# Expert gates: one-hots interleaved by two tokens, sixteen tokens an instruction, and gates stored token-innermost in chunks of 32

## What is computed

```python
idx = top-16 of (s_i + s_j) per head              # idx = i*128 + j, [t, 128 choices]
g   = softmax(best)                               # [t, 128]
a   = gelu(einsum('td,ted->te', xb, peer_u[idx]))
out = einsum('te,ted->td', (g * a), peer_v[idx])
```

## Time and profile before

| | |
|---|---|
| time, median of 3 runs | 4610.86 us (4606.46 to 4625.53) |
| profiled execution, its span | 4614.7 us |
| median against that span | 3.8 us below it |
| PE, DVE, ACT, POOL busy in the span | 3770.5, 3353.4, 1271.7, 989.7 us |
| up to `dense_gates` | 0 to 1976 us |
| `dense_gates` | 1976 to 2349 us, 373 us |
| `experts` | 2349 to 4562 us, 2213 us |
| `final_norm` | 4562 to 4614.7 us |

### The profile page before, as it was taken

One profiled execution on the slowest core, in us unless ns is written; L12 is line 12 of the kernel. 1 busy time (PEld: TensorE's weight loads), 2 busy tenths in 40 slices (PEclk: granted clock), 3 DMA queues, 4 the chain that ended last, 5 costly groups with the idle time before them and its releaser, 6 DMA issues. The chain is left out here.

```text
span 4614.7 us, 58881 instructions
## 1 busy us (share of the span) xinstructions
PE 3770.5 (82%) x19550; PEld 2045.0 (44%) x19550; DVE 3353.4 (73%) x5560; ACT 1271.7 (28%) x2566; POOL 989.7 (21%) x1048
## 2 busy tenths in 40 slices
PE   7946667997899233389989999999999999999994
PEld 3525543553455111156644444444444445444442
DVE  1043341222589799976659999999999999999998
ACT  2132132222233111133333333333333323333321
POOL 0000000000000000000024434443444444444444
PEclk9966588998999567655579999999999999999997
DMA  2200012101110100034478898898888888888885
GB/s 87 82 3 0 0 79 101 42 14 64 43 41 26 58 0 0 0 108 134 142 252 327 327 335 316 330 341 320 322 338 330 325 334 331 332 335 330 326 321 191
DMA packets 234207, 852.35 MB, mean 185 GB/s; under 512 B 15952, under 2 KB 115088, under 8 KB 162704
## 3 DMA queue, kind: packets, MB, share of 16 engines
q0 software_dynamic: 73728, 536.90, 30.9%
q1 hardware_dynamic: 160400, 314.42, 19.6%
HBM read 790.45 MB, written 60.82 MB: 184 GB/s over the span
## 5 line engine op out<-in xcount | busy, mean ns | idle before, releaser
L69 PE MATMUL x_ps_v<-x_v_hi,x_w_hi 128*128 128x512 f16 x1536 | 605.8, 394 | 134.5 <-DVE x_w_lo L1648 73.9
L1547 POOL DMA_INDIRECT x_rows<-in_peer_uv,x_index x512 | 589.9, 1152 | 408.1 <-POOL x_index L1544 393.1
L1618 DVE SCALAR_TENSOR_TENSOR acc<-x_rows,x_share,acc 128x1024 f32<-128x1024 f32 x512 | 655.3, 1280 | 0.0
L1702 PE MATMUL x_ps_a<-h_hi,x_u_hi 128*128 128x256 f16 (+1 forms) x2048 | 620.2, 327 | 16.7 <-ACT x_u_hi L1560 16.7
L1703 PE MATMUL x_ps_a<-h_lo,x_u_hi 128*128 128x256 f16 (+1 forms) x2048 | 620.1, 327 | 0.0
L1544 POOL COPY x_index<-expert 128x1 uint32 (+1 forms) x512 | 337.8, 660 | 1260.9 <-DVE acc L1618 868.3
L70 PE MATMUL x_ps_v<-x_v_lo,x_w_hi 128*128 128x512 f16 x1536 | 603.6, 393 | 0.0
L71 PE MATMUL x_ps_v<-x_v_hi,x_w_lo 128*128 128x512 f16 x1536 | 602.2, 392 | 0.0
L1571 ACT ACTIVATE x_dots<-x_dots 128x1 f32<-128x1 f32 x512 | 103.9, 203 | 1333.7 <-DVE x_dots L1636 1333.7
L1208 POOL TENSOR_TENSOR b_hits_iota<-b_hits_iota,top_i 128x2048 f16<-128x2048 f16 x10 | 38.4, 3842 | 1917.8 <-DVE b_hits_iota L1274 1917.8
L1636 DVE CUSTOM_DVE_ANT_0 x_rows<-h_lo,x_rows 128x1024 f32<-128x1024 f32 x256 | 312.5, 1221 | 121.1 <-DMA x_rows<-in_peer_uv,x_index 120.4
(11 more groups left out here) (279 smaller groups left out, 6747.9 us busy)
## 6 DMA issues: line engine op xcount, KB each, us to landing
x_u_st<-in_peer_u_t SPq DMA_DIRECT2D x128, 512.0 KB
x_v_st<-in_peer_v SPq DMA_DIRECT2D x128, 512.0 KB
gate_scratch<-g_out SPq DMA_DIRECT2D x24, 2048.0 KB, 8.7
x_gate<-gate_scratch SPq DMA_DIRECT2D x32, 1024.0 KB
x_gate<-gate_scratch SPq DMA_DIRECT2D x32, 512.0 KB, 4.2
m_w_st<-in_w_merge SPq DMA_DIRECT2D x8, 1536.0 KB, 6.4
k_w_st<-in_w_route SPq DMA_DIRECT2D x16, 576.0 KB, 3.7
x_rows<-in_peer_uv,x_index POOLq DMA_INDIRECT x512
```

Source lines behind the costliest of these rows:

```text
L69: pe.matmul(out, lhs_hi, rhs_hi, start=first, stop=False)
L1547: pool.indirect_dma_start(rows[:, m % RING], None, uv_all, bass.IndirectOffsetOnAxis(ap=index[:, m % RING:m % RING + 1], axis=0)).then_inc ...
L1618: dve.scalar_tensor_tensor(R.acc[:, DT + tile], rows[:, r, D:2 * D], share[:, s:s + 1], R.acc[:, DT + tile], ALU.mult, ALU.add).then_inc(v ...
L1702: pe.matmul(out, u_hi[:, e, ko], R.h_hi[:, ko, t], start=ko == 0, stop=False)
```

## The change

Every instruction of DVE now makes one-hots for sixteen tokens (`OCT` = 16), stored as eight pairs: within a pair the two tokens alternate, so a token's next key stands 2 f16 elements (4 bytes) further. `iota` holds each key twice only, and is read again for each pair. ACT writes the gates of a quad as four adjacent tokens of one i, and for that reads PSUM key by key, each time four tokens that stand 128 f32 apart. `out`, `R.g_dram` and `gate` keep 32 tokens of one expert side by side, so that line 1659 (1668 to 1670 in the changed kernel) reads runs of 32 adjacent f32.

```diff
+G_CHUNK = 32
...
-        OCT, RING, HALF_T, QUAD = 8, 3, 32, 4
+        OCT, RING, HALF_T, QUAD = 16, 3, G_CHUNK, 4
-        iota = sb("g_iota", [P, NKEYS, OCT], f16)
-        hot_i, hot_j = sb("g_hot_i", [P, NKEYS, OCT], f16), sb("g_hot_j", [P, RING, NKEYS, OCT], f16)
-        hot_g = sb("g_hot_g", [P, RING, 2, NKEYS, OCT], f16)
-        out = sb("g_out", [P, 2, N_GROUPS, HALF_T, I_GROUP], f32)
+        iota = sb("g_iota", [P, NKEYS, 2], f16)
+        hot_i = sb("g_hot_i", [P, OCT // 2, NKEYS, 2], f16)
+        hot_j = sb("g_hot_j", [P, RING, OCT // 2, NKEYS, 2], f16)
+        hot_g = sb("g_hot_g", [P, RING, 2, OCT // 2, NKEYS, 2], f16)
+        out = sb("g_out", [P, 2, NKEYS, HALF_T], f32)
...
-                    each = lambda ap: ap.rearrange("p (a t) -> p a t", a=1).to_broadcast([P, NKEYS, OCT])
-                    dve.tensor_tensor(hot_i[:], iota[:], each(R.ij[:, 0, toks]), ALU.is_equal).then_inc(i_ok, 1)
+                    shape = [P, OCT // 2, NKEYS, 2]
+                    each = lambda ap: ap.rearrange("p (m n t) -> p m n t", n=1, t=2).to_broadcast(shape)
+                    keys = iota[:].rearrange("p (m n) t -> p m n t", m=1).to_broadcast(shape)
+                    dve.tensor_tensor(hot_i[:], keys, each(R.ij[:, 0, toks]), ALU.is_equal).then_inc(i_ok, 1)
                     if not first or o >= RING:
-                        dve.wait_ge(mm, 2 * (NO * n + o - RING + 1))
+                        dve.wait_ge(mm, OCT // QUAD * (NO * n + o - RING + 1))
...
-                        t = QUAD * (q % 2) + u
-                        pe.matmul(ps[:, q % 4, u], hot_j[:, s, :, t], hot_g[:, s, 0, :, t], start=True, stop=False)
+                        m, t = divmod(QUAD * q % OCT + u, 2)
+                        pe.matmul(ps[:, q % 4, u], hot_j[:, s, m, :, t], hot_g[:, s, 0, m, :, t], start=True, stop=False)
...
-                    act.activation(out[:, h, :, t0:t0 + QUAD].rearrange("p g t f -> p t g f"),
-                                   ps[:, q % 4].rearrange("p t (g f) -> p t g f", f=I_GROUP), ACT.Copy).then_inc(ev, 1)
+                    act.activation(out[:, h, :, t0:t0 + QUAD], ps[:, q % 4].rearrange("p t n -> p n t"),
+                                   ACT.Copy).then_inc(ev, 1)
...
-                sp.dma_start(gate[:, t0:t0 + n_t], R.g_dram[i, :, t0:t0 + n_t]).then_inc(gate_in[b], 16)
+                part = slice(t0 // G_CHUNK, (t0 + n_t) // G_CHUNK)
+                sp.dma_start(gate[:, part], R.g_dram[i, :, part]).then_inc(gate_in[b], 16)
...
-                        dve.tensor_tensor(w[:, k % 2, 0:n_t], g_act[:, k % 2, 0:n_t], gate[:, t0:t0 + n_t, e],
-                                          ALU.mult).then_inc(w_ok, 1)
+                        chunks = lambda ap: ap.rearrange("p (c t) -> p c t", t=G_CHUNK)
+                        dve.tensor_tensor(chunks(w[:, k % 2, 0:n_t]), chunks(g_act[:, k % 2, 0:n_t]),
+                                          gate[:, t0 // G_CHUNK:(t0 + n_t) // G_CHUNK, e], ALU.mult).then_inc(w_ok, 1)
...
-        R.g_dram = nc.dram_tensor("gate_scratch", [N_GROUPS, P, ND, I_GROUP], f32).ap()
+        R.g_dram = nc.dram_tensor("gate_scratch", [N_GROUPS, P, ND // G_CHUNK, I_GROUP, G_CHUNK], f32).ap()
```

More of the change, by code:

```diff
@@ L1386, in _ @@
                     sp.wait_ge(ev, NQ * i + NQ // 2 * (h + 1))
-                    dst = R.g_dram[:, :, bass.ds(BODY * i + HALF_T * h, HALF_T)].rearrange("g j t f -> j g (t f)")
-                    sp.dma_start(dst, out[:, h].rearrange("p g t f -> p g (t f)")).then_inc(stored[h], 16)
+                    dst = R.g_dram[:, :, bass.ds(2 * i + h, 1)].rearrange("g j c f t -> j g (c f t)")
+                    sp.dma_start(dst, out[:, h].rearrange("p (g f) t -> p g (f t)", f=I_GROUP)).then_inc(stored[h], 16)
             for h in range(2):
@@ L1394, in _ @@
             dve.wait_ge(consts, 16)
-            dve.tensor_copy(iota[:], row[:].rearrange("p (n a) -> p n a", a=1).to_broadcast([P, NKEYS, OCT])
+            dve.tensor_copy(iota[:], row[:].rearrange("p (n a) -> p n a", a=1).to_broadcast([P, NKEYS, 2])
                             ).then_inc(i_ok, 1)
@@ L1402, in body @@
                     toks = bass.ds(BODY * n + OCT * o, OCT)
-                    each = lambda ap: ap.rearrange("p (a t) -> p a t", a=1).to_broadcast([P, NKEYS, OCT])
-                    dve.tensor_tensor(hot_i[:], iota[:], each(R.ij[:, 0, toks]), ALU.is_equal).then_inc(i_ok, 1)
+                    shape = [P, OCT // 2, NKEYS, 2]
+                    each = lambda ap: ap.rearrange("p (m n t) -> p m n t", n=1, t=2).to_broadcast(shape)
+                    keys = iota[:].rearrange("p (m n) t -> p m n t", m=1).to_broadcast(shape)
+                    dve.tensor_tensor(hot_i[:], keys, each(R.ij[:, 0, toks]), ALU.is_equal).then_inc(i_ok, 1)
                     if not first or o >= RING:
-                        dve.wait_ge(mm, 2 * (NO * n + o - RING + 1))
-                    dve.tensor_tensor(hot_j[:, s], iota[:], each(R.ij[:, 1, toks]), ALU.is_equal)
+                        dve.wait_ge(mm, OCT // QUAD * (NO * n + o - RING + 1))
+                    dve.tensor_tensor(hot_j[:, s], keys, each(R.ij[:, 1, toks]), ALU.is_equal)
                     dve.wait_ge(i_ok, NO * n + o + 2)
@@ L1417, in body @@
                 for q in range(NQ):
-                    o, s = q // 2, (NO * turn + q // 2) % RING
+                    o = q * QUAD // OCT
+                    s = (NO * turn + o) % RING
                     if not first or q >= 4:
                         pe.wait_ge(ev, NQ * n + q - 3)
-                    if q % 2 == 0:
+                    if q * QUAD % OCT == 0:
                         pe.wait_ge(hot_ok, NO * n + o + 1)
                     for u in range(QUAD):
-                        t = QUAD * (q % 2) + u
-                        pe.matmul(ps[:, q % 4, u], hot_j[:, s, :, t], hot_g[:, s, 0, :, t], start=True, stop=False)
-                        last = pe.matmul(ps[:, q % 4, u], hot_j[:, s, :, t], hot_g[:, s, 1, :, t], start=False, stop=True)
+                        m, t = divmod(QUAD * q % OCT + u, 2)
+                        pe.matmul(ps[:, q % 4, u], hot_j[:, s, m, :, t], hot_g[:, s, 0, m, :, t], start=True, stop=False)
+                        last = pe.matmul(ps[:, q % 4, u], hot_j[:, s, m, :, t], hot_g[:, s, 1, m, :, t],
+                                         start=False, stop=True)
                     last.then_inc(mm, 1)
@@ L1467, in experts @@
         v_hi, v_lo = sb("x_v_hi", [P, E, D], f16), sb("x_v_lo", [P, E, D], f16)
-        gate = sb("x_gate", [P, ND, E], f32)
+        gate = sb("x_gate", [P, ND // G_CHUNK, E, G_CHUNK], f32)
         g_act, w = sb("x_g_act", [P, 2, 512], f32), sb("x_w", [P, 2, 512], f32)
```

## The result

| | before | changed |
|---|---|---|
| time, median | 4612.43 us (4606.46 to 4625.53, 4 runs, one more than in the table above) | 4437.87 us (4430.75 to 4443.22, 4 runs) |
| profiled execution, span | 4614.7 us | 4428.9 us |
| `dense_gates`, first one-hot to the next stage's first load | 372.7 us | 241.2 us |
| `experts`, that load to the first of `final_norm` | 2213.4 us | 2160.5 us |

The changed kernel takes 0.9609 of the time (95% interval 0.9593 to 0.9624): 3.9% faster, 4438 us where 4420 was forecast. The profiled execution is the fastest of its four, so its stages are compared with stages, not with the median. Of its 185.8 us, 131.4 come from `dense_gates`, 52.9 from `experts`, and 1.5 lie in stages that the change doesn't touch.

The account below looks back on a forecast made before the run. PE was taken to bound `dense_gates`, DVE (waiting only for gathers) `experts`. From the 4614.7 us span, 131 and 62 us off gave 4422, forecast as 4420 us, 4.1% faster; own range 4400 to 4465.

Parts of the forecast that it names:

- PE at 0.107 us: In `dense_gates`, each matmul with keys 4 bytes apart was to take 0.107 us, where it took 0.233.
- a hop that costs 0.126: In `dense_gates`, 0.126 us of each matmul's 0.233 was put down to the next key standing 16 bytes on.
- DVE at 1226 ns, groups of 4.67 us: One-hots in `dense_gates`: 1226 ns per 2048-element instruction, 4.67 us per group of four outside the loop, 228 us in all.
- the rival's price: DVE takes one f16 at a time in `dense_gates`: 433 us of groups, 4627 us in all; DVE without pairs, chance 0.09.
- ACT at 0.8 us, hidden: In `dense_gates`, an eviction reading PSUM with hops was to take 0.8 us, where it took 598 ns, hidden by DVE's time.
- The bound of 0.94: Worst case for ACT's eviction in `dense_gates`, from DVE's hopping reads: 0.94 us, 3.8 us for a group's four.
- Stores at 8.7 us, hidden: In `dense_gates`, 24 stores of 2 MB, each landing 8.7 us after issue, 209 us, hidden under DVE's 228.
- The stage 131 us shorter: The last store of `dense_gates` was to come at 2208.3 instead of 2339.56: 131 us less.
- `experts` 62 us shorter: A faster line 1659 takes 75 us off DVE's work; with some of it lost to gather waits, 62 us gained.
- The lower bound: The smallest gain given for `experts`: 30 us, if DVE's waits for gathers grow by a third.
- a faster line 1659 elsewhere doesn't shorten the gather: In `experts`, DVE's 124.6 us of gather waits were placed where two visits follow each other, untouched by faster work elsewhere.
- 4420 against 4438: The forecast median, 4420 us: the sum on the span, 4422, with the median put 3.8 us below the span.

Follow-up runs that it names:

- tokens_apart: The changed kernel without interleaving, each token's 128 keys side by side, so DVE's key operand stands still inside: 4650.39 us.
- visits_spread: The changed kernel with the 16 visits of a group in `experts` dealt out otherwise, halving the places where two follow each other: 4444.21 us.
- ring_of_five: The changed kernel with a fifth slot in the ring of gathered rows and the loop's group written out five times: 4292.22 us.
- gates_loaded_once: The changed kernel without the loads of `gate` after the first group, so its output isn't the layer's: 4396.27 us, one execution.

## Why the prediction was right, and where not

- **PE at 0.107 us**: right, at half clock. The mechanism was too coarse: the prediction spoke of a hop that costs 0.126, the runs show a cost that grows with the step of the streamed operand, 0.118 us for 8 bytes at either clock and 0.230 to 0.234 for 16 at the only clock that they ran at, 0.50. 4 bytes cost what adjacent keys cost (`tokens_apart`), and DVE is the slower one. Taking 0.107 "since 4 bytes are nearer to 2 than to 16" was a choice between two bounds that came out right: by a straight line between them it would have been about 0.125.
- **DVE at 1226 ns, groups of 4.67 us**: right; 1217 to 1225 ns, and the first groups start at 1974.60 and 1979.27. The pairs held; `tokens_apart` shows that the rival's price (4627, with 433 us of groups, 446 with the stage's ends) would have been paid without them: 4650.39 and 447.6. The row behind that price was misread: POOL worked on the same tile beside every one of the ten instructions of line 1208, the fastest too, which began 0.05 us before POOL. The 2292 ns held all the same, in a stage where POOL is idle.
- **ACT at 0.8 us, hidden**: hidden, and too dear: 599 ns. The bound of 0.94 would have been too low for a hop on the other side (1103 ns, though starts are 0.88 apart). The Trainium skill, "Advanced Engine Details and Errata", section "PSUM Cachelines", speaks of matmuls; its slowdown did not carry over to ACT's reads here (599 ns against 598).
- **Stores at 8.7 us, hidden**: right; 24 of them, 8.7 us to landing in the changed kernel too.
- **The stage 131 us shorter**: 131.4.
- **`experts` 62 us shorter**: the mechanism was right and the term mis-sized. DVE's work fell by 75.6 us (75 forecast), but the waits for gathers grew by 24.1, not by 13. (The lower bound was a slip of 3 us too: waits a third longer leave 33, not 30.) They vary: in nine profiled executions with the new layout, the old ring and the old order of visits they are 135.0 to 157.8 us (mean 148.2), and `experts` lasts 2149 to 2172; in the two with the old layout 124.6 and 127.2. The step that failed is "a faster line 1659 elsewhere doesn't shorten the gather", with the waits put down to two visits in a row. `visits_spread` refutes the second half. What stands in its place, by `ring_of_five` and the table of landings: a gather has only the time of the visits ahead in the ring to land; with four slots that is 8.4 us for landings of 7.5 on average and 10.5 at most, and less work for DVE shortens it (8.6 before), wherever it lies. The landings grew as well, from 7.2 us; that other transfers lengthen them fits `gates_loaded_once` (6.9). ACT's wait for `x_v_st` rose from 6.8 to 73.3 us in the changed kernel, but it is 79.1 in `ring_of_five`, where DVE hardly waits, so it is not what held DVE.
- **4420 against 4438**: of the 18 us, 9 are that term (62 less 52.9) and 9 the distance of the profiled execution after (4428.9) from the median of its runs, which lies above it, where the prediction had put it 3.8 us below. That term was no more than where one profiled execution of the kernel before happened to fall among its runs. The rest, 1.5 us in stages that were not touched and the 2 us by which 4420 is under the sum on the span, cancels.

## What to carry to other kernels

Read PE's pace from the distance of two starts and compare it with a matmul of the same shape elsewhere in the trace; where it is longer, look at the step of the streamed operand first (here 4 bytes cost nothing, 8 and 16 did), and keep two f16 side by side for DVE while you shorten it. When an edit takes work off an engine that also waits for transfers, expect part of it to come back as waiting (here 24 of 76 us), and before you call that bandwidth, compare a gather's time from issue to landing with the time from issue to its use, and give the ring one more slot: here a fifth gave 139 us on top of the 186 that the whole change gave, and more than twice what the change gave in `experts` (53).

## What the hardware showed that I had not expected

- A 128-column f16 matmul whose streamed operand steps 16 bytes takes 0.230 to 0.234 us (at a granted clock of 0.50, the only one seen), with 8 bytes 0.118 at either clock, with 4 bytes 0.0576 at full clock and 0.107 at half, as adjacent; the loaded operand's step of 16 bytes shows only as 0.063 against 0.0576 at full clock.
- ACT reads PSUM with a hop of 512 bytes at every element at 599 ns for 512, as it reads adjacent ones (597); writing with a hop of 128 bytes takes 1103 ns, with starts 0.88 us apart.
- In `experts`, the ring of four left 149 us of waits at 334 GB/s; the ring of five 0.9 us at 357, with gathers that land no sooner (7.6 us against 7.5).
